# A division moved up, level operands made one level ahead, and two gate projections cut in pieces

## The reference, cut to what matters

```
# mLSTM, per chunk of a head: the division by the larger of |den| and exp(-m)
den = w_inter[..., None] * (q n) + sum(s)
h = num / jnp.maximum(jnp.abs(den), jnp.exp(-m_t))[..., None]
out = head_rmsnorm(h, norm_w) * sigmoid(o) @ w_out
...
# HGRN2, per head: decays between positions t and s
decay = jnp.exp(jnp.where(mask[:, :, None], bc[t] - bc[s], NEG))
a = jnp.einsum('bhtd,bhsd,bhtsd->bhts', qc, kc, decay)
o = head_rmsnorm(qc * exp(bc) @ state + a @ v, norm_w) * silu(g)
y = o @ w_out
```

## Time and profile before

| | |
|---|---|
| median of three runs | 1936.68 us (1935.5 to 1940.43) |
| the profiled execution | 1943.37 us, its span 1941.5 us |
| mean granted clock of PE | 0.993 |
| PE busy | 1898.2 us (98%) |
| DVE, ACT, POOL busy | 917.0, 576.1, 729.8 us |
| mLSTM stage's output part | about 539 to 592 us of the span |
| HGRN2 stage | about 1003 to 1341 us of the span |

### The profile page before, as it was taken

The page is one execution under the profiler, slowest core; times in us unless marked ns, Lnnn a source line. Parts: engine busy times, 40 slices in busy tenths (PEclk is TensorE's granted clock), DMA queues, the critical chain, the costliest instruction groups (busy, mean ns, idle before and its releaser), DMA issues. The chain is left out here.

```text
span 1941.5 us, 36854 instructions
## 1 busy us (share of the span) xinstructions
PE 1898.2 (98%) x15078; PEld 1626.5 (84%) x15078; DVE 917.0 (47%) x1225; ACT 576.1 (30%) x1226; POOL 729.8 (38%) x625
## 2 busy tenths in 40 slices
PE   9999999999999999999999999999999999999997
PEld 8778744888887888888867888767999999999996
DVE  3898687667565444444336777765200000000023
ACT  1443213455522111110036657533121211111102
POOL 6755422555644434444527777652200000000011
PEclk9999999999999999999999999999999999999999
DMA  9213750322215666631212111102957568778893
GB/s 333 88 55 146 274 193 31 99 83 76 82 44 189 211 208 216 216 121 60 103 66 67 67 67 66 57 12 83 330 198 249 198 226 288 252 268 323 330 366 120
DMA packets 82824, 313.58 MB, mean 162 GB/s; under 512 B 10121, under 2 KB 10641, under 8 KB 82529
## 3 DMA queue, kind: packets, MB, share of 16 engines
q1 hardware_dynamic: 75952, 289.73, 42.3%
q0 software_dynamic: 4464, 14.35, 2.2%
q10 hardware_dynamic: 2241, 7.14, 1.0%
HBM read 301.43 MB, written 9.75 MB: 160 GB/s over the span
## 5 line engine op out<-in xcount | busy, mean ns | idle before, releaser
L261 PE MATMUL banks<-sb_act,sb_ring 128*64 128x112 f32 (+9 forms) x5088 | 624.9, 301 | 3.4 <-issue 2.3
L261 PEld LDWEIGHTS banks<-sb_act,sb_ring 128*128 128x128 f32 (+1 forms) x5088 | 594.3, 174 | 27.8 <-issue 8.0
L261 PE MATMUL banks<-sb_x_norm,sb_ring 128*128 128x256 f32 (+3 forms) x1616 | 332.6, 406 | 2.9 <-ACT sb_ring L468 2.0
L261 PEld LDWEIGHTS banks<-sb_x_norm,sb_ring 128*128 128x128 f32 (+1 forms) x1616 | 242.9, 171 | 67.1 <-issue 30.2
L3722 DVE TENSOR_TENSOR sb_act<-sb_work,banks 128x192 f32<-128x192 f32 (+7 forms) x88 | 27.1, 308 | 494.4 <-PE banks L261 475.7
L443 POOL TENSOR_TENSOR sb_ring<-sb_ring 128x512 f32<-128x512 f32 x146 | 206.6, 1415 | 101.1 <-PE banks L261 52.9
L261 PE MATMUL banks<-sb_work,sb_ring 128*64 128x256 f32 (+2 forms) x1124 | 231.7, 407 | 2.0 <-ACT sb_ring L468 1.8
L261 PEld LDWEIGHTS banks<-sb_work,sb_ring 128*128 128x128 f32 (+1 forms) x1124 | 155.3, 165 | 56.6 <-issue 33.5
L3253 POOL DMA_INDIRECT sb_work<-first_expert_rows,sb_table x8 | 7.5, 937 | 443.1 <-DMA first_expert_rows<-sb_x_norm 441.0
L3524 ACT ACTIVATE sb_work<-banks 128x192 f32<-128x192 f32 (+7 forms) x88 | 25.8, 294 | 300.0 <-PE banks L261 277.7
L499 POOL TENSOR_TENSOR sb_act<-sb_act,sb_ring 128x256 f32<-128x256 f32 x75 | 71.7, 956 | 67.0 <-ACT sb_act L468 59.5
(11 more groups left out here) (529 smaller groups left out, 2584.8 us busy)
## 6 DMA issues: line engine op xcount, KB each, us to landing
sb_ring<-in_w_moe_up SPq DMA_DIRECT2D x176, 512.0 KB
sb_ring<-in_w_moe_down SPq DMA_DIRECT2D x64, 704.0 KB
sb_act<-in_cond_w SPq DMA_DIRECT2D x84, 512.0 KB, 3.7
sb_ring<-in_w_ffn_up SPq DMA_DIRECT2D x44, 512.0 KB
sb_ring<-in_w_h_in SPq DMA_DIRECT2D x32, 512.0 KB
sb_ring<-in_w_in SPq DMA_DIRECT2D x28, 512.0 KB
sb_ring<-in_w_m_in SPq DMA_DIRECT2D x24, 512.0 KB
sb_ring<-in_w_ffn_down SPq DMA_DIRECT2D x16, 704.0 KB
```

Of the source, the lines that this page charges most:

```text
L261: last = m.nc.tensor.matmul(out[part], weights[:, part], act, start=start, stop=stop, skip_group_check=skip)
```

## The change

- mLSTM: on DVE the last head's `divide` comes before `quads.sum_chunk(1)`; on PE the P6 piece of feature 2 comes behind the norm product and P7 of the second quad, that of feature 3 behind `with_head(3)`. The scaling of the next stage's first block goes from one POOL instruction to eight ACT activations behind `take_bias`.
- HGRN2 levels: DVE makes the late operand of level j + 1 between the take and the adds of level j - 1, where it made that of level j in front of the take.
- HGRN2 gates: the two projections are issued in four pieces each; ACT takes them at (6, 7) and (7, 3), where it took them at (6, 5) and (7, 2). PE issues a piece before the level's product.
- HGRN2 weight differences of the output stage: POOL makes 2 and 6 of them in heads 6 and 7 and 8 behind, where it made 4, 7 and 5.

```
@@ Unnormed
+    def scale_tiles(self, m, act):
+        act.wait_ge(self.steps, BIASED)
+        first = self.norm.scale_at
+        for k in range(KD):
+            w = self.w[:, rows(k, P)]
+            last = m.nc.scalar.activation(w, w, ACT.Copy, scale=m.mod[:, first + k:first + k + 1])
+        last.then_inc(self.steps, 1)
@@ stage_m, PE
-                quads.product(pe, 0, P6, (k,))
...
             norms[HEADS - 1].pe(m, pe)
             quads.product(pe, 1, P7)
+            quads.product(pe, 0, P6, (2,))
             with_head(3)
+            quads.product(pe, 0, P6, (3,))
@@ stage_m, ACT
             unnormed.take_bias(m, act)
+            unnormed.scale_tiles(m, act)
             squares(6, KD)
@@ stage_m, POOL
             for k in range(KD - 1):
-                if k == KD - 2:
-                    unnormed.scale_weights(m, pool)
                 norm_out.add(m, pool, k)
@@ stage_m, DVE
             finish(HEADS - 2)
+            divide(HEADS - 1)
             quads.sum_chunk(dve, 1)
-            divide(HEADS - 1)
             finish(HEADS - 1)
@@ tables
-H_LAST = {(6, 5): ("g", 6), (7, 2): ("g", 7)}
+H_LAST = {(6, 4): ("g", 6, 0, 3), (6, 5): ("g", 6, 3, 4), (6, 6): ("g", 6, 4, 6), (6, 7): ("g", 6, 6, 8),
+          (7, 0): ("g", 7, 0, 2), (7, 1): ("g", 7, 2, 4), (7, 2): ("g", 7, 4, 7), (7, 3): ("g", 7, 7, 8)}
+H_TAKEN = {(6, 7): ("g", 6), (7, 3): ("g", 7)}
...
-    MADE_6 = {4: (0, T1), 5: (0, T3), 6: (1, T1), 7: (1, T3)}
-    MADE_7 = {1: (0, T2), 2: (1, T2), 3: (0, T4), 4: (1, T4), 5: (2, T1), 6: (2, T3), 7: (3, T1)}
-    MADE = [(3, T3), (2, T2), (3, T2), (2, T4), (3, T4)]
+    MADE_6 = {5: (0, T1), 7: (0, T3)}
+    MADE_7 = {1: (1, T1), 3: (1, T3), 4: (0, T2), 5: (1, T2), 6: (0, T4), 7: (1, T4)}
+    MADE = [(2, T1), (2, T3), (3, T1), (3, T3), (2, T2), (3, T2), (2, T4), (3, T4)]
@@ stage_h, PE
+            def project_part(kind, h, first, last):
+                b = at[kind, h]
+                if first == 0:
+                    plan.wait_loaded(m, pe, b)
+                    pe.wait_ge(m.evac, plan.done + b - 1)
+                for k in range(first, last):
+                    made = in_strips(m, ps[:, b % 2, :], m.ring[:, plan.slot(b), rows(k, P)], m.HN[:, k, :], k == 0,
+                                     k == KD - 1)
+                if last == KD:
+                    made.then_inc(m.blocks_done, 1)
...
                     if (h, j) in H_LAST:
-                        project(*H_LAST[h, j])
+                        project_part(*H_LAST[h, j])
@@ stage_h, ACT: take of (h, j) in H_TAKEN behind keep(h, 3) and keep(h, 7)
-                if (h, 2) in H_LAST:
-                    take(*H_LAST[h, 2])
-                    load_exponentials()
...
+                if (h, 3) in H_TAKEN:
+                    take(*H_TAKEN[h, 3])
+                    load_exponentials()
@@ stage_h, POOL
-                        if j == 5:
-                            pool.wait_ge(head_out, 2 * EARLY)
-                            pool.wait_ge(m.blocks_done, plan.done + plan.n)
...
+            pool.wait_ge(head_out, 2 * EARLY)
             for made in MADE:
@@ stage_h, DVE
+            times(0, 1)
             for h in range(HEADS):
                 q, k = q_of(h), k_of(h)
-                times(h, 1)
                 if h == 0:
                     sums(1)
                 else:
                     take(h - 1, LEVELS - 1)
+                times(h, 2)
                 step(nc.vector.memset(atts[h % 2], 0.0))
                 take(h, 0)
...
                     if j > 1:
-                        times(h, j)
                         take(h, j - 1)
+                        if j < LEVELS - 1:
+                            times(h, j + 1)
+                        elif h + 1 < HEADS:
+                            times(h + 1, 1)
                         add(h, j - 1)
```

More of the change, by code:

```diff
@@ L2561 @@
            (("f", 7), ("q", 6)), (("v", 6), ("v", 7)), (("g", 5), ("q", 7))]
-H_LAST = {(6, 5): ("g", 6), (7, 2): ("g", 7)}
-H_BLOCKS = H_FIRST + [block for pair in H_PAIRS for block in pair] + list(H_LAST.values())
+H_LAST = {(6, 4): ("g", 6, 0, 3), (6, 5): ("g", 6, 3, 4), (6, 6): ("g", 6, 4, 6), (6, 7): ("g", 6, 6, 8),
+          (7, 0): ("g", 7, 0, 2), (7, 1): ("g", 7, 2, 4), (7, 2): ("g", 7, 4, 7), (7, 3): ("g", 7, 7, 8)}
+H_TAKEN = {(6, 7): ("g", 6), (7, 3): ("g", 7)}
+H_BLOCKS = H_FIRST + [block for pair in H_PAIRS for block in pair] + list(H_TAKEN.values())
 H_BESIDE = [[2, 2, 2, 1, 2, 2, 2, 1]] * 6 + [[2, 2, 2, 1, 0, 0, 0, 0], [0] * 8]
@@ L2884, in _ @@
                 keep(h, 5)
-                if (h, 5) in H_LAST:
-                    norms[h - 1].square(m, act)
-                    take(*H_LAST[h, 5])
-                    load_exponentials()
                 ahead(h, 5)
                 keep(h, 6)
-                if h and (h, 5) not in H_LAST:
+                if h:
                     norms[h - 1].square(m, act)
@@ L2894, in _ @@
                 keep(h, 7)
+                if (h, 7) in H_TAKEN:
+                    take(*H_TAKEN[h, 7])
+                    load_exponentials()
             take_cross(HEADS - 1)
@@ L2954, in _ @@
                         quads.combine(pool, *MADE_6[j])
-                    if h == HEADS - 1:
-                        if j == 5:
-                            pool.wait_ge(head_out, 2 * EARLY)
-                            pool.wait_ge(m.blocks_done, plan.done + plan.n)
+                    if h == HEADS - 1 and j in MADE_7:
                         quads.combine(pool, *MADE_7[j])
                 combine(h, LEVELS - 1)
+            pool.wait_ge(head_out, 2 * EARLY)
             for made in MADE:
```

## The result

The changed kernel took 1940.53 us (median of 20 runs, 1937.4 to 1943.72), the kernel before, run beside it, 1936.37 us (20 runs, 1934.4 to 1940.84). The ratio is 1.0019, with a 95% interval of 1.0013 to 1.0025: 2.5 to 4.8 us slower, where the forecast said 1.5 us faster. That lies within the 0.3% that was called "the same", but it is on the other side of zero, and the interval excludes the forecast.

What follows compares the result with a forecast made beforehand. TensorE, busy 98% of the span, was taken as the bound, with gains only in its waits and slow clock. -4.2 + 5.7 - 3.3 + 0.3 = -1.5 us gave a median of 1935.2 us; 8-in-10 range 1926 to 1943 us.

Steps and rivals of the forecast that it cites:

- The mLSTM tail, -4.2 us: mLSTM stage's end: earlier division removes a 2.35 us wait and its slow stretch, -4.0; scaling on ACT, -0.2 us.
- The slow clock in the sum (1.7 us): PE behind the mLSTM tail's 2.35 us wait: 20 matmuls at the lower clock lose 1.7 us, which would go.
- Level operands one level ahead, +5.7 us: HGRN2 heads: the moved DVE product delays the adds, so PE waits longer at P6: +5.7 us (+2.5 to +9.5).
- The upper bound, +9.5: HGRN2 heads: upper end of the range +2.5 to +9.5 us for making level operands one level ahead.
- 4 x 0.7 = 2.8: Heads 2 to 5, before the cross products: DVE's longer chain adds 0 to 1.5 us each, taken as 0.7.
- 2.0 us above my figure: HGRN2 levels: if DVE operations with two SBUF inputs and POOL exclude one another, the whole change ends 2.0 us higher.
- Gate projections in pieces, -3.3 us: Heads 6 and 7: projection pieces fill PE's waits of 2.94 and 2.91 us, less new waits: -3.3 us (-8.0 to -1.0).
- 9.0 - 1.6 - 2.4 - 1.7: Heads 6 and 7: 9.0 us filled, less waits before first piece (1.6) and cross products (2.4), and slow clock (1.7).
- POOL's late differences, +0.3 us: Output stage: eight weight differences after the levels can delay the last head's norm product by 0 to 0.9 us.
- POOL does not get in the way: Rival, HGRN2 heads: the add is late only by the product's 0.42 us; -12.8 us, 1924 us; chance 0.25.
- The clock falls in the heads too: Rival, heads 1 to 5: P6 waits of about 1.5 us bring the slow clock, +8.5 us, 1943.7 us; chance 0.13.
- The first part doesn't do what it says: Rival, mLSTM tail: the norm product waits for something besides the division, 4.0 us stay, 1939.2 us; chance 0.05.

Runs made afterwards that it cites:

- first profile of before: The unchanged kernel before, profiled once for the forecast: 1943.37 us, span 1941.5 us.
- the kernel with the adds first: The changed kernel with DVE's Strassen adds ahead of the product made one level ahead: 1944.19 us, 8.0 us above the kernel before.
- second profile of before: The unchanged kernel before, profiled once more: 1934.92 us, one run.
- the four profiles with these waits: Two profiles of the unchanged kernel before (1943.37 and 1934.92 us), and one each of it with the mLSTM part alone and with the scaling on ACT alone.
- The thin projections: The kernel before, its last two gate projections multiplying only the first of eight features (4 matmuls for 32): 1940.10 us, +1.9 us against before.
- the hold at level 4: The changed kernel with adds before the product, and POOL's level 4 difference held until DVE's cross operands are made: 1933.20 us, -3.4 us against before.
- one number, -4 us: The kernel before with the mLSTM part alone, finishing work of heads 0 to 4 moved to levels 5 and 6: 1928.64 us, -7.9 us against before.
- the kernel with POOL held for the adds: The changed kernel, with POOL waiting at level 3 until DVE has made both adds: 1964.26 us, +28.5 us against before.
- the kernel with the adds first and the finish later: The changed kernel with adds before the product and both finish halves of heads 0 to 4 at level 5: 1941.06 us, +4.5 us against before.

## Why the prediction was wrong, by its own steps

The forecast was -1.5 us, the result is +4.2. If the parts add up as they were timed, the 5.7 us between them are 0.6 for the mLSTM part (-3.6 for -4.2), 2.8 for the level operands (+8.5 for +5.7) and 2.3 for the pieces with POOL's differences (-0.7 for -3.0). Two steps failed: the term of the level operands was too small, and the waits that the pieces were to fill moved instead.

In each of three profiles the stretches between the same matmuls (us; from the last head's counts, L1837 or L1845, to the feed-forward network, the HGRN2 stage up to level 0 of head 6, from there to the cross products of head 7, from there to the router):

| stretch | first profile of before | second | changed |
|---|---|---|---|
| mLSTM tail | 57.58 | 55.93 | 50.93 |
| heads 0 to 5 | 230.01 | 230.03 | 237.99 |
| heads 6 and 7 | 51.77 | 48.82 | 48.04 |
| output stage | 45.97 | 45.99 | 46.97 |

**The mLSTM tail, -4.2 us: right.** Alone it measured -3.6 us. The wait of 2.35 and the one of 0.48 us went, nothing took their place. The slow clock in the sum (1.7 us) is there in some executions and not in all: of the seven profiles that keep the wait, four show it behind (20 matmuls in 5.21 to 6.17 us), three don't (4.48 us).

**Level operands one level ahead, +5.7 us: right mechanism, term too small.** It measured +8.5 us alone, and the stretch of heads 0 to 5, which is the same in both profiles of before to 0.02 us, grew by 7.96 us. The upper bound, +9.5, held it. Head 1 grew by 1.17 us, as forecast (+1.2). Heads 2 to 5 have 1.53, 1.68, 1.52 and 1.40, together 6.1 where the sum had 4.5 with the gate pairs, and head 0 has 0.67, which the sum left out.

The part that I had taken at half its bound came out right: the waits before the cross products are 1.03, 0.45, 1.03 and 0.44 us, 2.95 together, where the sum had 4 x 0.7 = 2.8. Too small was the rest. The P6 waits of heads 2 to 5 grew by 1.19 or 1.20 us each while those of 0.67 to 0.72 us before level 5 went, 2.0 us net for the four heads, where I had 0.3 a head; ACT's late parts early in heads 3 and 5 make waits of 0.69 and 0.43 us, where I had 0.5 for the two; and there is head 0. The forecast's remark that by the Trainium skill's rule the result would be 2.0 us above my figure doesn't follow from its own bounds: four times 1.5 - 0.7 is 3.2 us, and +9.5 stands 3.8 above +5.7. It also gave that rule (page "SBUF — State Buffer", section "Who interferes with whom") without its exception: the page says that operations with one SBUF input don't contend only of those outside the two-port modes. A row where one was held up is in the last section. What I did not see is that this is not the sum of a wait at P6 and one at the cross products but one DVE chain, as the kernel with the adds first showed.

**Gate projections in pieces, -3.3 us: here the mechanism failed.** "9.0 - 1.6 - 2.4 - 1.7": the two new waits are right (1.67 for 1.6 and 2.33 for 2.4 us). But the 9.0 us took for granted that the two holes would be filled, and a third wait of 1.97 us opened before level 3 of head 7, where I had put 0.5 us and called it nothing net. The waits of the stretch went from 6.44 or 6.74 us in the two profiles of before to 5.97, 0.5 to 0.8 us less where the sum had 1.9. The slow clock is a second, smaller error, since it is a matter of chance: 3.2 of the 9.0 us were slow clock, which the four profiles with these waits have between 0 and 3 us long (1.4 on average), and the 1.7 us against it did not come in the changed kernel's profile. In that profile the stretch is 0.8 us shorter than in the quickest profile of before and 2.1 shorter than the mean of the four; by the runs the pieces with POOL's differences are worth -0.7 us given the rest, and +3.8 us alone. The thin projections show why: PE's work is not what sets the length of these levels.

**POOL's late differences, +0.3 us: small but off.** They cost 1.0 us, just over the upper bound of 0.9.

The four stretches of the table sum to -5.0 + 8.0 - 0.8 + 1.0 = +3.2 us from the second profile of before to the changed kernel, against +4.2 us by the medians; a slow stretch of 1.6 us in the tail of the second profile is in this difference.

**The reference execution.** I set the sum against a profiled execution 6.7 us above the median and took its slow stretches as a lasting part of the kernel. Against the second profile, the same working gives 5.9 - 1.6 - 2.4 - 1.7 = 0.2 us of gain for the pieces in place of 3.3, and +1.6 us for the sum. With the average of the four profiles it gives 1.6 us of gain and +0.2 us for the sum. So the choice of the reference explains some 2 to 3 us of the miss, and the terms above the rest.

**The rivals.** "POOL does not get in the way": excluded (1.15 us for the add, and the hold at level 4, which brought three stretched operations back to 0.42 and 0.56 us). "The clock falls in the heads too": the P6 waits came out at 1.36 to 1.40 us, as it supposed, but the matmuls behind all five take 1.95 to 1.97 us as before, and the window behind one of them has 1.00. With waits of 2.05 to 2.08 us, in the kernel with the adds first, it does fall in three heads of four. "The first part doesn't do what it says": excluded.

## What to carry to other kernels

Before filling a hole in the bounding engine's time, ask whether that engine sets the length of the stretch: if its operands come late, the hole moves with the work. Leaving work out is a quick test. A wait can be a fence: making an operand earlier released POOL into DVE's critical chain, and keeping POOL out, or taking work that nobody needs yet out of that chain (one number, -4 us), made the kernel faster where the whole change made it slower. And a slow stretch of the clock in one profile is a sample; take a second profile before it enters a sum.

## What the runs showed of the hardware that was not expected

Behind waits of 2.94 and 2.91 us the granted clock of PE fell to 0.50 in one execution of the kernel before and stayed at 1.00 in another, with both waits equal to 0.01 us. Over all profiles it fell behind 2.94 us in three of five, behind 2.90 or 2.91 us in one of five, behind the 2.33 to 2.35 us of the mLSTM tail in four of seven, and behind the 2.05 to 2.08 us of the kernel with the adds first in three heads of four. It stayed at 1.00 behind 2.33 and 1.97 us in the changed kernel. Behind the waits of 3.95 to 3.99 us of the kernel with POOL held for the adds, the 16 or 32 matmuls that follow took 2.93, 3.48, 3.33, 3.68 and 3.68 us where 1.95 to 1.97 is usual, all five times:

```profile
1196.87 3.68 PE L261 MATMUL banks<-sb_work,sb_ring 128*64 128x256 f32 x16 [3.99 <-ACT sb_ring L468]
```

A DVE operation with one wide SBUF operand (and one value per partition) can be held up beside POOL too: in the kernel with the adds first and the finish later, the first scaling of the cross operands takes 1.32 us, where 0.29 us is usual, while POOL's weight difference runs from 1112.06 to 1113.33 us:

```profile
1112.06 1.27 POOL L443 TENSOR_TENSOR sb_ring<-sb_ring 128x512 f32<-128x512 f32 x1
1112.10 1.32 DVE L3093 TENSOR_SCALAR sb_work<-sb_work 128x128 f32<-128x128 f32 x1
```

The Trainium skill, page "SBUF — State Buffer", section "Who interferes with whom", says that a `tensor_scalar` operation can run in a mode with both ports, and then contends with GpSimd as well. The 1.32 us agree with that; no run shows whether this operation was in that mode. My forecast had counted only the operations with two operands.
